# Norm factors and running sums of a two-block transformer: spread over partitions by transfers through memory

## What is computed

```
def rmsnorm(x, g):
    y = x * rsqrt(mean(x * x, axis=-1) + EPS)      # one factor per token
    return y * g
```

```
decay[s, t] = exp(min(a[s] - max(0, max over r <= t of a[r]), 0))   for s <= t, else 0
a[s] = input gate[s] - cumulative sum of log forget gates[s]
```

## Time and profile before

| | |
|---|---|
| median of three runs | 1630.93 us (1629.58 to 1631.39) |
| span of the profiled execution | 1627.0 us; it has no time of its own beside the span |
| TensorE busy | 1602.6 us, 98% |
| VectorE busy | 1093.6 us, 67% |
| ScalarE busy | 924.1 us, 57% |
| GpSimd busy | 41.3 us, 3% |
| moved by the DMA engines | 285.48 MB, mean 175 GB/s |
| granted TensorE clock | full speed in all slices |

### The profile page before, as it was taken

One profiled execution on the slowest core, in us unless ns is written; L12 is line 12 of the kernel. 1 busy time (PEld: TensorE's weight loads), 2 busy tenths in 40 slices (PEclk: granted clock), 3 DMA queues, 4 the chain that ended last, 5 costly groups with the idle time before them and its releaser, 6 DMA issues.

```text
span 1627.0 us, 23976 instructions
## 1 busy us (share of the span) xinstructions
PE 1602.6 (98%) x9451; PEld 1361.8 (84%) x9451; DVE 1093.6 (67%) x1763; ACT 924.1 (57%) x1557; POOL 41.3 (3%) x77
## 2 busy tenths in 40 slices
PE   8999999999999999999999999999999999999998
PEld 6887888878788888888887788888888889788887
DVE  5877776778667777665676466567666667675665
ACT  5755754566665556644576555456454474574544
POOL 3000000000020000000001000000000000000000
PEclk9999999999999999999999999999999999999999
DMA  8444666545355555655554265564655564356552
GB/s 292 143 143 146 228 216 200 187 156 169 98 188 193 184 190 177 199 185 192 183 166 134 74 206 188 189 187 157 218 188 187 181 194 146 117 169 195 192 184 75
DMA packets 210114, 285.48 MB, mean 175 GB/s; under 512 B 9596, under 2 KB 178830, under 8 KB 210004
## 3 DMA queue, kind: packets, MB, share of 16 engines
q1 hardware_dynamic: 208356, 280.00, 53.3%
q0 software_dynamic: 1648, 3.97, 0.7%
HBM read 282.72 MB, written 3.43 MB: 176 GB/s over the span
## 4 chain that ended last, share of the span: by engine, by line
PE 91%; DVE 4%; ACT 4%; issue 1%; DMA 0%; SPq 0%; DVEq 0%; ACTq 0%
PE two L2104 84%; DVE w_lo L1387 2%; ACT w_hi L791 1%; PE two L2179 1%; PE two L2360 1%; PE two L2694 1%; PE two L2370 1%; PE two L2347 1%; ACT p_sb L976 1%; PE two L2461 0%; PE two L2680 0%; DMA raw<-in_mem_w_kv 0%; DVE aux L1593 0%; ACT act_parts L838 0%; PE two L2165 0%
## 5 line engine op out<-in xcount | busy, mean ns | idle before, releaser
L2104 PE MATMUL two<-act_parts,w_hi 128*128 128x512 f32 (+1 forms) x2784 | 801.7, 353 | 1.4 <-ACT act_parts L1169 1.4
L1387 DVE TENSOR_TENSOR w_lo<-raw,w_hi 128x1024 fp32r<-128x1024 f32 (+1 forms) x520 | 612.8, 1220 | 116.3 <-ACT w_hi L791 115.6
L2104 PE MATMUL two<-act_parts,w_lo 128*128 128x256 f32 x2256 | 635.0, 281 | 0.0
L2104 PEld LDWEIGHTS two<-act_parts,w_hi 128*128 128x128 f32 x2784 | 487.0, 188 | 83.0 <-issue 6.6
L791 ACT CAST w_hi<-raw 128x1024 fp32r<-128x1024 f32 (+1 forms) x520 | 516.6, 1050 | 4.9 <-DMA raw<-in_ffn_w_up 3.3
L2104 PEld LDWEIGHTS two<-act_parts,w_lo 128*128 128x128 f32 x2256 | 425.5, 189 | 2.1
L2104 PE MATMUL two<-w_hi,act_parts 128*128 128x512 f32 (+2 forms) x832 | 250.5, 378 | 5.0 <-DVE w_lo L1387 2.7
L916 ACT COPY p_sb<-two 128x512 f32<-128x512 f32 x108 | 62.4, 578 | 247.9 <-PE two L2104 247.9
L2104 PE MATMUL two<-w_hi,hid_even 128*128 128x512 f32 x576 | 189.3, 394 | 0.6
L2104 PEld LDWEIGHTS two<-w_hi,act_parts 128*128 128x128 f32 x832 | 150.6, 188 | 38.8 <-issue 7.0
L1513 DVE TENSOR_TENSOR pt_sb<-two,p_sb 128x512 f32<-128x512 f32 x54 | 37.3, 691 | 198.9 <-ACT p_sb L916 198.9
(11 more groups left out here) (312 smaller groups left out, 1208.3 us busy)
## 6 DMA issues: line engine op xcount, KB each, us to landing
raw<-in_ffn_w_up SPq DMA_DIRECT2D x160, 512.0 KB, 3.9
raw<-in_ffn_w_down SPq DMA_DIRECT2D x132, 512.0 KB, 3.6
raw<-in_ffn_w_gate SPq DMA_DIRECT2D x80, 512.0 KB, 3.5
raw<-in_a_w_in SPq DMA_DIRECT2D x24, 512.0 KB, 4.7
raw<-in_fox_w_in SPq DMA_DIRECT2D x20, 512.0 KB, 3.8
raw<-in_ffn_w_up SPq DMA_DIRECT2D x32, 256.0 KB, 3.2
raw<-in_w_kv SPq DMA_DIRECT2D x12, 512.0 KB, 3.6
raw<-in_mem_w_kv SPq DMA_DIRECT2D x8, 512.0 KB, 11.2
```

Of the source, the lines that this page charges most:

```text
L1387: nc.vector.tensor_tensor(w_lo[:, r, 0:n], raw[:, r, 0:n], w_hi[:, r, 0:n], ALU.subtract).then_inc(lo_done, 1)
L2104: return nc.tensor.matmul(dst, a, w, start=start, stop=stop, skip_group_check=True)
```

## The change

Nine spreads of the norm's factor and four of the running maximum leave TensorE. In their place GpSimd issues transfers: per norm two writes of `rx` (128 numbers, one from each partition) into a row of `rx_dram`, then, when both have landed, a read of that row of 1 KB into all 128 partitions of `rstd`. VectorE's nine copies go, and it waits for the transfer (`rstd_ready`) before the first use instead. For the running maximum GpSimd writes the four rows to `row_dram` and reads all 4 KB into each partition of `run_rows`, which lies on `stack_b`, the memory of `hid_odd`, unused at that time. `decays(h)` reads it from SBUF, and `decays(0)` moves behind the split of slot 22. TensorE no longer waits for `decays`.

```
@@ gpsimd @@
+            def spread_rstd(key):
+                n = SPREAD.index(key)
+                for b in range(NTB):
+                    pool.wait_ge(rx_done, 2 * NORMS[key][2] + b + 1)
+                    pool.dma_start(rx_dram[n, b * P:(b + 1) * P], rx[:, b]).then_inc(rx_out, 16)
+                pool.wait_ge(rx_out, 32 * n + 32)
+                pool.dma_start(rstd[:, :], spread(rx_dram[n, :], SEQ)).then_inc(rstd_in, 16)
+
+            spread_rstd("a")
+            pool.wait_ge(gates_m, 1)
+            pool.dma_start(row_dram, rowc[0:A_HEADS, :]).then_inc(row_out, 16)
+            pool.wait_ge(row_out, 16)
+            pool.dma_start(run_rows, bass.AP(tensor=row_dram.tensor, offset=row_dram.offset, ap=[[0, P], [SEQ, A_HEADS], [1, SEQ]])).then_inc(rows_in, 16)
             for h in range(A_HEADS):
                 pool.wait_ge(ml_e, h + 1)
...
+            spread_rstd(0)
             pool.wait_ge(relb_in, 32)
             nc.gpsimd.memset(relb[0:P - CHUNK, :, P + CHUNK:2 * P], NEG).then_inc(vec_const, 1)
+            spread_rstd("kv")
 
             pool.wait_ge(acc_full, 4 * EV["band"] + 4)
             gain_row(final_g)
+            spread_rstd(1)
...
             gain_row(norm_g_2[0, 1])
+            spread_rstd(2)
             make_taps(CCH - 1)
...
+            for p, row, key in ((2, norm_g_2[0, 5], 3), (3, norm_g_2[1, 1], 4), (4, norm_g_2[1, 3], "fox"), (5, norm_g_2[1, 5], 5)):
                 pool.wait_ge(hg_done, 4 * p)
                 gain_row(row)
+                spread_rstd(key)
@@ vector, feed-forward @@
                 splits(first + 9)
-                dve.wait_ge(rstd_ps, SPREAD.index(f) + 1)
-                step(nc.vector.tensor_copy(rstd[:, :], acc[0][0][:, 0:SEQ]))
                 out_of(0)
                 out_of(1)
+                rstd_ready(f)
@@ vector, first mixer @@
-                dve.wait_ge(ml_bc, h + 1)
+                dve.wait_ge(rows_in, 16)
+                if h < 2:
+                    dve.wait_ge(h_pt, PAIR0["a_mem"] + h + 1)
                 if h >= 2:
                     dve.wait_ge(ml_e, h - 1)
-                bc = st[:, 0:SEQ]
+                bc = run_rows[:, h, :]
...
-            dve.wait_ge(rstd_ps, SPREAD.index("a") + 1)
-            nc.vector.tensor_copy(rstd[:, :], bank[0][:, 0:SEQ]).then_inc(a_rstd, 1)
-            dve.wait_ge(a_rstd, 1)
             splits(17)
+            rstd_ready("a")
             a_logs()
...
             taps_qk("AQ0")
-            decays(0)
             take_qk("AK0", bank[4])
             splits(21)
             o_lo("a_mem", 0)
             splits(22)
+            decays(0)
             decays(1)
@@ vector, "kv" and "fox" @@
-            dve.wait_ge(rstd_ps, SPREAD.index("kv") + 1)
-            step(nc.vector.tensor_copy(rstd[:, :], bank[6][:, 0:SEQ]))
             splits(116)
+            rstd_ready("kv")
...
-            dve.wait_ge(rstd_ps, SPREAD.index("fox") + 1)
-            step(nc.vector.tensor_copy(rstd[:, :], acc[0][0][:, 0:SEQ]))
             splits(429)
...
             f_rows()
+            rstd_ready("fox")
@@ tensor @@
-            def spread_rstd(key, dst):
-                for b in range(NTB):
-                    pe.wait_ge(rx_done, 2 * NORMS[key][2] + b + 1)
-                    ins = nc.tensor.matmul(dst[:, b * P:(b + 1) * P], rx[:, b:b + 1].to_broadcast([P, P]), ident[:, :],
-                                           start=True, stop=True, skip_group_check=True)
-                ins.then_inc(rstd_ps, 1)
...
-            def spread(h):
-                if h:
-                    pe.wait_ge(ml_x, h)
-                else:
-                    pe.wait_ge(gates_mm, 1)
-                nc.tensor.matmul(st[:, 0:SEQ], ident[0:A_HEADS, h:h + 1].to_broadcast([A_HEADS, P]), rowc[0:A_HEADS, :],
-                                 start=True, stop=True).then_inc(ml_bc, 1)
```

More of the change, by code:

```diff
@@ L287, in build @@
         fox_parts = sb("fox_parts", [P, 2, 4, SEQ], F32R)
+        row_dram = nc.dram_tensor("row_dram", [A_HEADS, SEQ], F32, kind="Internal").ap()
+        rx_dram = nc.dram_tensor("rx_dram", [len(SPREAD), SEQ], F32, kind="Internal").ap()
         tab_dram = nc.dram_tensor("tab_dram", [B_HEADS, 512], F32, kind="Internal").ap()
@@ L315, in build @@
         rstd_c = qk[:, 5, :]
+        run_rows = stack_b[:, :].rearrange("p (h t) -> p h t", h=A_HEADS)
         def tap_cols(c, g):
@@ L436, in build @@
         fp_taken = sem("fp_taken")
-        rstd_ps = sem("rstd_ps")
-        a_rstd = sem("a_rstd")
+        rx_out = sem("rx_out")
+        rstd_in = sem("rstd_in")
         ff_raw = sem("ff_raw")
@@ L485, in build @@
         gates_em = sem("gates_em")
-        ml_bc = sem("ml_bc")
+        row_out = sem("row_out")
+        rows_in = sem("rows_in")
         ml_x = sem("ml_x")
@@ L776, in _ @@
             gain_row(norm_g_2[0, 3])
-            for p, row in ((2, norm_g_2[0, 5]), (3, norm_g_2[1, 1]), (4, norm_g_2[1, 3]), (5, norm_g_2[1, 5])):
+            for p, row, key in ((2, norm_g_2[0, 5], 3), (3, norm_g_2[1, 1], 4), (4, norm_g_2[1, 3], "fox"), (5, norm_g_2[1, 5], 5)):
                 pool.wait_ge(hg_done, 4 * p)
                 gain_row(row)
+                spread_rstd(key)
         @block.scalar
@@ L1393, in root_x, with rstd_ready @@
                 nc.vector.reciprocal(rx[:, b:b + 1], ssx[:, b:b + 1]).then_inc(rx_done, 1)
+            def rstd_ready(key):
+                dve.wait_ge(rstd_in, 16 * SPREAD.index(key) + 16)
             def rx_ready(key, b):
@@ L2269, in ffn @@
                 first_project(("ffn", f), 1, f)
-                spread_rstd(f, acc[0][0])
                 turn_hid(0)
@@ L2495, in a_out @@
                 out_chunk("a", a_ready, i, b)
-            spread_rstd("a", bank[0])
             for g in range(4):
@@ L2510, in _ @@
             pe.wait_ge(cw_done, 1)
-            pe.wait_ge(a_rstd, 1)
             scores("a_mem", 0)
@@ L2523, in _ @@
             turns("a_mem", 1)
-            spread(0)
             pe.wait_ge(pj_free[1], GI["VO0"] + 1)
@@ L2527, in _ @@
             values("a_mem", 1)
-            spread(1)
             part("AQ1", bank[5], 1)
-            spread(2)
             pe.wait_ge(fp_taken, PI["AQ0"] + 1)
             part("AK1", bank[2], 0)
-            spread(3)
             part("AK1", bank[2], 1)
@@ L2595, in _ @@
             first_project("VA", 1, "kv")
-            spread_rstd("kv", bank[6])
             band_part("QM", bank[7], 0)
@@ L2795, in _ @@
             first_project("FV0", 1, "fox")
-            spread_rstd("fox", acc[0][0])
             project("FVB", 0)
```

## The result

The changed kernel takes **1638.45 us** (median of 5 runs, 1634.47 to 1638.91), the kernel before beside it 1629.58 (1629.32 to 1631.39): ratio 1.0045, 95% interval 1.0034 to 1.0056. It is 0.45% slower by that ratio (8.9 us, 0.54%, by the two medians) where 0.2% faster was forecast, and above the range. The profiled execution took 1636.34 us with a span of 1634.6, 7.6 more than the span before; three of the timed runs took 2.1 to 2.6 us more, at a mean clock of 0.995 to 0.996 against its 0.998, so the profile accounts for most of the loss, not for all. The clock alone does not order the runs: the fastest, 1634.47, also shows 0.996.

What follows compares the result with a forecast made beforehand. TensorE was taken as the bound, with 91% of the chain. Savings of 2.64 us at the feed-forward norms and 1.3 in the first mixer made 3.9, from 1630.93 to 1627.0 us; range 1623.6 to 1631.0.

Steps and rivals of the forecast that it cites:

- The spreads in the feed-forwards: Six feed-forward norms: TensorE's spreads, 0.44 us each and all on the path, go; 2.64 us saved.
- The wait on `rstd`: Norms: write and broadcast take 6.7 us (4.2 to 12.7) against 11.4 us of cover in the last feed-forward; cost 0.
- The bytes: Norm transfers: some 1.7 MB against 285 MB moved, 0.6%; cost 0.
- What GpSimd has queued behind the spreads: GpSimd's queue: tap products and slope tables are hundreds of us early, the next gain row a layer early; cost 0.
- The mixer's transfers and VectorE's chain: First mixer: rows land at 77.4, 1.0 us to spare; VectorE's chain, and so TensorE, comes 1.3 us earlier.
- TensorE's idle time: First mixer: TensorE, relieved of 3.4 us, waits 2.1 us for ScalarE's activation before the keys-and-queries product.
- The port rule weighed at the mixer's write: First mixer: VectorE's scalings could delay GpSimd's write up to 1.3 us, making the term 0.9 in place of 1.3.
- The span: Profiled span 1627.0 us against median 1630.93; 3.9 us lie around the span, and the sum is carried to the median.
- The slower one: Rival: both mixer transfers at their upper bound, rows at 82.7; 1631.3 us, or 1633.9 with issues held up; chance 0.08.

Runs made afterwards that it cites:

- turned_ffn: Kernel before with running sums and only the six feed-forward norms (turned into 128-byte pieces) by transfers, VO1's second half before keys-and-queries, taps before norm 1: 1623.48 us.
- norms_only: Changed kernel with the first mixer's running sums spread by TensorE again, all nine norms still by transfers: 1637.51 us.
- both_mended: Changed kernel with tap products held until feed-forward 1 has used its gate, and VO1's second half ahead of the keys-and-queries product: 1628.47 us.
- taps_later: Changed kernel with GpSimd's tap products and slope tables held until the gate of feed-forward 1 has been used: 1630.76 us.
- sums_swap: Kernel before with only the running sums by transfers, and VO1's second half ahead of the keys-and-queries product: 1625.23 us.
- taps_first: Changed kernel with the spread of norm 1 put behind GpSimd's tap products: 1637.37 us.
- turned_best: Changed kernel with all nine norms' factors turned by VectorE into 128-byte pieces, VO1's second half before keys-and-queries, taps before norm 1: 1624.74 us.
- wide_writes: Changed kernel with each write sending 512 bytes from one partition, an identity row in place of the norm factors: 1628.61 us.

## Why the prediction was wrong, point by point

- **The spreads in the feed-forwards, 2.64 us: right.** Where nothing stands in the way they bring 0.2 to 0.5 each, 2.3 in turned_ffn. In the changed kernel five of six kept them.
- **The wait on `rstd`, 3 + 3.5 with 0.2 for two waits, 6.7 us, "so 0": wrong in size, and at "kv" in what stands behind it.** It took some 15 us, above the upper bound of 12.7; the write of single numbers alone took 8.6, and up to 12.1. The bound came from transfers made of rows, a kind that does not bound this one. "I read the same cover or more at the other norms" was true of the cover, 11.9 us at "kv", but what to do beyond it was argued for a feed-forward alone. There TensorE's lead covers even 15 us (not in norms_only's profile); at "kv" TensorE needs that very product. The row read for TensorE there is another matmul's, which stands some 10 us ahead (368.3 and 378.65 in the changed kernel). Cost 1.6, and 4.0 in both_mended.
- **The bytes, 0.6%, "0": wrong.** The share of bytes says nothing of pieces of 4 bytes. The weights beside them come later, and at the start TensorE waits 1.28 us for one. Elsewhere in the changed kernel's profile no new wait of TensorE for weights shows it.
- **What GpSimd has queued behind the spreads, "hundreds of us early", 0: wrong, and the largest step.** Early for whoever uses the tap products, but the step asked only who waits for them, not what they run beside. Moved 22.7 us, they held a VectorE instruction for 7 us, and TensorE idled 3.8 us: 3.9 on the stage in the profile, and 7.7 in the medians between the changed kernel and taps_later.
- **The mixer's transfers and VectorE's chain: right,** with the landing forecast to 0.1 us, in part by luck: the write took 2.8 and not 3.1, the waits 0.54 and not 0.2. So was TensorE's idle time, "2.1 us", measured 2.41. **Its price was wrong:** it was counted as idle time that cost nothing more, and the clock fell behind it. The stage came out 1.8 longer and not 1.3 shorter; sums_swap shows the 1.3 with the idle time filled.
- **The port rule weighed at the mixer's write** did not bite there: GpSimd issued at 72.31, 0.29 after `rowc` was ready, while VectorE's four scalings ran from 72.14, and neither took longer (0.54 and 1.14 us); whether the scalings ran in the two-port mode the trace does not tell. The same page bites in feed-forward 1. "SBUF — State Buffer", section "Who interferes with whom", of the Trainium skill says that a VectorE instruction with two inputs in SBUF contends with a GpSimd instruction that reads SBUF, and that the order of issue decides who blocks. The trace agrees that they contend and that either side can lose (8.44 for 1.26; 4.49 for 2.35). It shows two things more: VectorE's instructions with one input in PSUM went free beside the same products (2.16 us for eight), and VectorE did not get in between GpSimd's instructions of 0.58 us each, it waited until all twelve were done.
- **The span.** The 3.9 us that "lie around the span" compare the span of one execution with the median of others. In the runs on record the time is 1.7 to 2.9 us above the span, 1.8 in most. Nothing in the forecast hung on it.
- **The rivals.** The slower one had the wait in the mixer, and took 0.08. The kernel was slower by four other mechanisms (half clock behind TensorE's idle time, the late row at "kv", the meeting with the tap products, the late weight slot at the start), none of which was on the list; each was a step costed at 0.

The parts of the loss in the changed kernel's profile: mixer 1.8, "kv" 1.6, feed-forward 1 3.9, start 2.0 (1.3 a late weight slot, the rest open), less 1.6 saved in the other five feed-forwards: 7.7 of the 7.6 measured.

## What to carry to other kernels

When work is put into a queue, ask of everything behind it not only who waits for it but beside what it will now run; long runs of GpSimd instructions that read SBUF belong where VectorE's next instructions are not awaited. A column of single numbers should be turned into rows on the chip before it goes to memory. Idle time of a TensorE that bounds the kernel can have two prices, its own length and that of the half clock behind it, so a freed gap is filled by exchanging the next independent work into it, or the change can be worth less than nothing.

## What the runs showed of the hardware that was not expected

- One VectorE instruction of 0.35 to 0.42 us with both inputs in SBUF held for 7.2 us (after) and 6.87 us (norms_only) beside twelve back-to-back GpSimd products. Started the other way round (taps_later), GpSimd's four products took 4.49 us in place of 2.35. Beside the same twelve, VectorE's instructions with one input in PSUM took their usual time (before).
- 128 numbers of 4 bytes, one per partition, to memory: 8.6 us median, 12.1 at most (after), 14.2 for GpSimd's wait in a busy refill (taps_first); 8 pieces of 128 bytes (turned_best) and one of 512 bytes (wide_writes): 1.7 us. A broadcast of 1 KB into 128 partitions took 5.2 to 7.7 us (the medians of the kernels), more than one of 4 KB rows (4.1 to 4.4).
- 2.41 us without work on TensorE, after a long busy stretch, were followed by 6.8 us at 1.2 GHz; 2.43 us at "kv" by 3.4 us (both_mended); 1.85 us at "kv" by 3.4 in turned_best, and 1.83 us at the same place by none in the changed kernel. In its feed-forward 1 even 2.66 us were followed by full speed (granted clock 1.00 from 488 to 496). So between 1.8 and 2.7 us the length of the gap alone does not decide.
